# A transformer block with expert retrieval: the middle group's mixer spread over more tiles, and the score loads moved to ScalarE's DMA queue

## What is computed

```python
h = modulate(rmsnorm(x), shift1, scale1)
qa, ka, va, qb, kb, vb, ga, gb = split(h @ w_in)
y_sb = stick_breaking_attention(qa, ka, va)          # 8 heads, strictly causal
y_sw = sliding_window_sink_attention(qb, kb, vb)     # 8 query heads, 2 chunks of 64
x = x + gate1 * ((sigmoid(ga) * (y_sb @ sb_proj) + sigmoid(gb) * (y_sw @ sw_proj)) @ w_out)
h2 = modulate(rmsnorm(x), shift2, scale2)
# per token and head (8): scores against 2 x 128 sub-keys, top 16 of each,
# top 16 of the 256 sums, softmax over them
x = x + gate2 * sum_k gate_k * gelu(h2 . U[e_k]) * V[e_k]      # 128 experts of a token
out = rmsnorm(x)
```

## Time and profile before

| | |
|---|---|
| time, median of 3 runs | 3500.83 us (3499.89 to 3506.99) |
| the profiled execution's own time | 3481.42 us |
| its span | 3479.6 us |
| first gather starts | 378.0 us |
| busy: TensorE, VectorE, ScalarE, GpSimd | 2187.0, 2024.9, 1152.5, 1121.8 us |
| moved by DMA | 1274.27 MB, 366 GB/s over the span |

### The profile page before, as it was taken

How to read it: one execution, slowest core, us unless ns; L and a number is a source line. 1 busy time by engine, 2 the same in 40 slices (tenths; PEclk the granted TensorE clock), 3 DMA queues, 4 the chain that set the end, 5 groups by cost and what they waited for, 6 DMA issues and landing times.

```text
span 3479.6 us, 35550 instructions
## 1 busy us (share of the span) xinstructions
PE 2187.0 (63%) x11116; PEld 979.8 (28%) x11116; DVE 2024.9 (58%) x4779; ACT 1152.5 (33%) x3650; POOL 1121.8 (32%) x1033
## 2 busy tenths in 40 slices
PE   5878677668976856777667877774433443344333
PEld 2566533244433412232233432341100000000000
DVE  1021556665655465777586667556666666666644
ACT  2111335642222235666543223222322232223222
POOL 0000133323322232444333333333344344434442
PEclk9999888889987978988888988886665565665655
DMA  9433679988999898999999999999999999999998
GB/s 367 171 133 111 258 296 367 357 330 347 372 371 394 332 419 326 416 390 396 368 370 412 421 421 385 392 420 421 392 421 421 421 399 421 421 421 391 421 421 335
DMA packets 197214, 1274.27 MB, mean 366 GB/s; under 512 B 21192, under 2 KB 38632, under 8 KB 54048
## 3 DMA queue, kind: packets, MB, share of 16 engines
q0 software_dynamic: 147616, 1074.03, 75.7%
q1 hardware_dynamic: 49408, 197.96, 14.6%
HBM read 1247.51 MB, written 24.40 MB: 366 GB/s over the span
## 4 chain that ended last, share of the span: by engine, by line
PE 40%; DMA 35%; ACT 10%; issue 9%; DVE 5%; POOL 1%; SPq 0%; POOLq 0%; DVEq 0%; ACTq 0%
DMA arena<-in_uv,idx_r 26%; PE pb L969 13%; PE pb L752 5%; PE pb L684 5%; ACT dg L1206 3%; PE pb L714 3%; ACT L105 2%; PE pb L687 2%; PE pb L773 2%; DMA arena<-in_w_ada 2%; DMA arena<-in_w_q 2%; PE pb L955 2%; DVE arena L1524 2%; PE pb L848 1%; PE pb L659 1%
## 5 line engine op out<-in xcount | busy, mean ns | idle before, releaser
L606 POOL DMA_INDIRECT arena<-in_uv,idx_r x1024 | 1118.7, 1093 | 2329.7 <-PE pb L969 1719.5
L1524 DVE CUSTOM_DVE_ANT_0 arena<-arena 128x1024 f32<-128x1024 f32 x1024 | 1249.3, 1222 | 743.1 <-DMA arena<-in_uv,idx_r 703.6
L969 PE MATMUL pb<-arena,dg 128*32 128x512 f32 x4096 | 735.3, 855 | 866.6 <-ACT dg L1206 866.6
L969 PEld LDWEIGHTS pb<-arena,dg 128*32 128x32 f32 x4096 | 134.3, 138 | 1357.0 <-ACT dg L1206 1060.9
L1200 ACT ACTIVATE gl<-dots 128x4 f32<-128x4 f32 x256 | 52.4, 205 | 989.0 <-DVE dots L1524 987.9
L752 PE MATMUL pb<-arena 128*128 128x384 f32 (+1 forms) x768 | 250.7, 484 | 66.2 <-issue 51.8
L105 ACT ACT_TABLE_LOAD x177 | 227.1, 1283 | 133.1 <-DVE dots L1524 77.0
L684 PE MATMUL pb<-arena 128*128 128x384 f32 (+1 forms) x768 | 238.8, 465 | 15.9 <-DMA arena<-in_w_mg 15.2
L1206 ACT ACTIVATE dg<-ig,gl 128x32 f32<-128x32 f32 x1024 | 245.1, 310 | 8.4 <-ACT gl L1200 0.2
L1195 ACT ACTIVATE ig<-istack,gate_r 128x32 f32<-128x32 f32 x1024 | 241.6, 308 | 0.0
L752 PEld LDWEIGHTS pb<-arena 128*128 128x128 f32 x768 | 153.6, 205 | 158.6 <-issue 95.1
(11 more groups left out here) (156 smaller groups left out, 2232.4 us busy)
## 6 DMA issues: line engine op xcount, KB each, us to landing
arena<-in_w_mg SPq DMA_DIRECT2D x24, 1536.0 KB, 10.8
arena<-in_w_ada SPq DMA_DIRECT2D x12, 2048.0 KB, 17.3
arena<-in_w_q SPq DMA_DIRECT2D x24, 1024.0 KB, 12.7
arena<-in_uv,idx_r POOLq DMA_INDIRECT x1024, 12.0
arena<-in_w_qk SPq DMA_DIRECT2D x12, 1024.0 KB, 13.6
arena<-in_w_out SPq DMA_DIRECT2D x3, 4096.0 KB, 16.2
arena<-in_w_sw SPq DMA_DIRECT2D x3, 3072.0 KB, 11.6
arena<-in_x SPq DMA_DIRECT2D x16, 512.0 KB, 15.2
```

Source lines behind the costliest of these rows:

```text
L606: pool.indirect_dma_start(ring[:, i % RING, :], None, uv, bass.IndirectOffsetOnAxis(ap=idx_r[:, b % 2, 4 * n + c:4 * n + c + 1], axis=0)). ...
L969: m = pe.matmul(pb[32 * c:32 * c + 32, VACC + i, :], dg[:, STEP * n // 4 % 2, c, :], ring[:, (STEP * g + c - first) % RING, D + i * HALF:D ...
L1524: dve.tensor_tensor_reduce(u, h2rep[:, slot(b, c), :], u, 1.0, 0.0, ALU.mult, ALU.add, dots[:, i % 8:i % 8 + 1]).then_inc(dots_done, 1)
```

## The change

Three numbers of the plan and one generator change.

1. `RATES` goes from (1.9, 2.9, 1.9) to (1.9, 2.5, 2.1): group 1's stages from H to OUT are spread over more tiles, group 2's over fewer. Group 2's start is no longer fixed at tile 235 but follows 2 tiles after group 1's end.
2. `SPREAD = (4.7, 8.0, 9.0)` sets the tiles that one head of PREP takes. Before they followed from the rate: 4.7, 4.7 and 7.1.
3. Selection of chunk n starts at tile 32n - 52 (`LEAD`) in place of 32n - 64, if the scores are ready in the plan by then.
4. The load of a chunk's scores is a row of ScalarE's program, 10 tiles ahead of the selection in place of 1.5, or 1.5 tiles ahead of it when the scores are just ready.

Places in the plan, in tiles:

| | before | after |
|---|---|---|
| group 1: H, QK, SWP, MG, OUT, PREP | 0, 15.4, 78.6, 109.4, 155.0, 181.6 | 0, 17.2, 89.2, 124.4, 177.2, 206.8 |
| group 2: H, QK, SWP, MG, OUT, PREP | 235, 256.4, 389.6, 434.7, 504.2, 540.6 | 272.8, 292.5, 413.8, 455.0, 517.8, 551.6 |
| group 2 ends | 599 | 624 |
| chunk 8 (first of block 2): selected from, to | 194.3, 224.3 | 224.1, 254.1 |
| chunk 9: selected from, to | 224.0, 254.0 | 240.1, 270.1 |
| load of chunk 8, load of chunk 9 | 192.8, 222.5 | 222.6, 238.6 |

```diff
-RATES = (1.9, 2.9, 1.9)
+RATES = (1.9, 2.5, 2.1)
+SPREAD = (4.7, 8.0, 9.0)
+LEAD = 52
...
-            self.now = begins[g]
+            self.now = begins[g] if g < len(begins) else self.now + 2
...
-                self.item("PREP", g, h, 18 * part)
-            self.now += 2
+                self.item("PREP", g, h, SPREAD[g] * RATES[g])
...
-        at = Plan([-probe("PREP", 0, 2) - 36, 0.0, 235.0])
+        at = Plan([-probe("PREP", 0, 2) - 36, 0.0])
...
+        def ready_at(b, m):
+            return at("PREP", GROUP[b], 2 * m + 1, part(GROUP[b], 11) + 4)
+
         def topk_at(b, m):
             n = CHUNKS * b + m
-            ready = at("PREP", GROUP[b], 2 * m + 1, part(GROUP[b], 11) + 4)
-            return ready if n < 2 else max(32.0 * (n - 2), ready)
+            return ready_at(b, m) if n < 2 else max(32.0 * n - LEAD, ready_at(b, m))
...
-                            yield topk_at(b, m) - 1.5
+                            yield max(topk_at(b, m) - 10, ready_at(b, m) - 1.5)
                             done = 16 * (HEADS // 2 * GROUP[b] + m + 1)
-                            sp.wait_ge(s_st[0], done)
-                            sp.wait_ge(s_st[1], done)
+                            act.wait_ge(s_st[0], done)
+                            act.wait_ge(s_st[1], done)
                             if n >= 2:
-                                sp.wait_ge(tk_used, n - 1)
-                            sp.dma_start(tk[:, n % 2, :], ...).then_inc(in_tk[n % 2], 16)
+                                act.wait_ge(tk_used, n - 1)
+                            act.dma_start(tk[:, n % 2, :], ...).then_inc(in_tk[n % 2], 16)
```

More of the change, by code:

```diff
@@ L542, in parked @@
                                      ssb[h % 2][:, 0:GB].rearrange("p b q n -> p b (q n)")).then_inc(s_st[h % 2], 16)
[L544 to L549, removed]
-                            yield topk_at(b, m) - 1.5
-                            done = 16 * (HEADS // 2 * GROUP[b] + m + 1)
-                            sp.wait_ge(s_st[0], done)
-                            sp.wait_ge(s_st[1], done)
-                            if n >= 2:
-                                sp.wait_ge(tk_used, n - 1)
-                            sp.dma_start(tk[:, n % 2, :], s_dram[b, :, 2 * m:2 * m + 2, :].rearrange("p h n -> p (h n)")).then_inc(in_tk[n % 2], 16)
                 def blocks():
@@ L582, in finals @@
                         sp.dma_start(out[b * P:(b + 1) * P, :], yfin).then_inc(stored, 16)
-                interleave(start(), mods(), first_weights(), mixer(0), parked(0), keys(), blocks(), finals(), *[s for g in range(1, GROUPS) for s in (mixer(g), parked(g))])
+                interleave(start(), mods(), first_weights(), mixer(0), parked(0), blocks(), finals(), *[s for g in range(1, GROUPS) for s in (mixer(g), parked(g))])
                 sp.wait_ge(stored, 16 * NB)
@@ L1173, in gates, with keys @@
                                            pb[:, MISC, 0:64].rearrange("p (c a n) -> p c a n", c=4, a=2)[:, :, 1], ACT.Copy).then_inc(pub_g, 1)
+                def keys():
+                    for b in range(NB):
+                        for m in range(CHUNKS):
+                            n = CHUNKS * b + m
+                            if n == 0:
+                                continue
+                            yield max(topk_at(b, m) - 10, ready_at(b, m) - 1.5)
+                            done = 16 * (HEADS // 2 * GROUP[b] + m + 1)
+                            act.wait_ge(s_st[0], done)
+                            act.wait_ge(s_st[1], done)
+                            if n >= 2:
+                                act.wait_ge(tk_used, n - 1)
+                            act.dma_start(tk[:, n % 2, :], s_dram[b, :, 2 * m:2 * m + 2, :].rearrange("p h n -> p (h n)")).then_inc(in_tk[n % 2], 16)
                 def replicate():
@@ L1217, in final @@
                         act.activation(stats[:, 50:51], stats[:, 49:50], ACT.Sqrt).then_inc(fin_rstd, 1)
-                interleave(start(), gates(), replicate(), gelus(), final(), *[mixer(g) for g in range(GROUPS)])
+                interleave(start(), keys(), gates(), replicate(), gelus(), final(), *[mixer(g) for g in range(GROUPS)])
             @block.vector
```

## The result

| | before | changed |
|---|---|---|
| median | 3503.90 us, 4 runs (3499.89 to 3506.99) | 3425.84 us, 4 runs (3419.07 to 3428.72) |
| ratio, 95% interval | | 0.9775 (0.9755 to 0.9795) |
| profiled execution, span | 3481.42, 3479.6 us | 3426.72, 3424.9 us |
| first gather | 378.0 us | 380.3 us |

The two profiled executions differ by only 54.7 us. All medians are of executions in the fast state; a single one, 5929.01 us in the experiment at rate 2.4, was in the slow state and is left out.

What follows compares the result with a forecast made beforehand. Taken as bound by bytes at 420 GB/s plus 243 us lost time; 34 + 16 + 5 + 4 - 12 - 8 - 2 = 37 us less, so 3500.8 - 37 = 3464 us, range 3430 to 3505.

Steps and rivals of the forecast that it cites:

- 1.4 us won per tile moved into such a stretch: Engine-bound stretches: a tile adds 1.2 us, saves 2.6 elsewhere; 34 us won in group 1's H to OUT.
- The first 142 us: Group 1's H, V and wait for its first weights: under 2 tiles moved, so 0 won of 43.3 lost.
- 16 for PREP: Group 1's PREP grows from 37 to 64 tiles, query weights no longer waited for: 16 us won, 7 left lost.
- The 8 us for tile 256: GpSimd waits for tile 256's indices, then chunk 9's 24 rows stand in one piece: 8 us lost, 24 if uncovered.
- The two waits of ScalarE: At chunk 8's and 9's loads ScalarE waits 11 us twice for stores; covered by gathers, otherwise 22 us lost.
- rival (c): Slower: ScalarE's two store waits empty the queue in group 1's PREP; about 3534 us, 3507 with half the stalls; chance 0.12.
- -12 and +5: Group 2, H to OUT: 12 us lost for 25 fewer tiles, 5 won as chunk 10's score wait goes.
- The runs' median lies 19.4 us above that execution: Whole kernel: offset between profiled execution and timed runs carried along, so 3444 us profiled became 3464 us.
- (b): Large win: group 1 falls to group 2's loss of 0.15 us per tile, group 2 pays nothing; about 3436 us; chance 0.17.
- (a): Small win: a tile costs its path 2.0 us, group 2 pays what group 1 gains; about 3496 us; chance 0.17.
- (d): Clock: thinner mixer idles TensorE; group 1's MG and PREP clock falls from 0.95 to 0.8; about 3495 us; chance 0.04.
- (e): Whole kernel: nothing moves, since only the bytes count; chance 0.03 at most.

Runs made afterwards that it cites:

- experiment at rate 2.4: Changed kernel with group 2's rate raised from 2.1 to 2.4: 3429.05 us, ratio 0.9786 to the kernel before.
- plan alone: Kernel before with only the new rates, PREP's spread and group 2's start, loads still on SyncE, selection 64 tiles ahead: 3430.64 us, 0.9855; repeated 3429.44, 0.9844.
- 2.7: Kernel before with group 1 at rate 2.7 and eight tiles per head of its PREP, group 2 at 1.9, loads on SyncE: 3474.41 us, 0.9906.
- 2.5: Kernel before with group 1 at rate 2.5 and eight tiles per head of its PREP, group 2 at 1.9, loads on SyncE: 3466.19 us, 0.9890.
- PREP alone: Kernel before with eight tiles in place of 4.7 per head of group 1's PREP, group 1 staying at rate 2.9: 3495.60 us, 0.9975.
- its variants: Changed kernel with chunk 8's selection in 18 tiles, 3416.25 us; or with rates 1.9, 2.4, 2.0, spread 4.7, 7, 8 and chunk 8 in 22 tiles, 3461.59.
- The two experiments in which half the change was made: Kernel before with only the new rates, spread and group 2 start, 0.9855; or with only loads on ScalarE, 10 tiles ahead where scores allow, 0.9975.

## Why the prediction was wrong

**The frame held.** Bytes at 420 GB/s plus lost time gives both profiles; the sum of the ledger (54.5) is the difference of the profiled executions (54.7).

**The term that was mis-sized: "and so 1.4 us won per tile moved into such a stretch".** H to OUT of group 1 won 48.4 us in place of 34. In this pair it is 24 tiles more and 48.4 us less lost, 2.0 us a tile. The plan alone, set against the kernel before at the same level, gives 1.9. The step behind the term, 1.2 us of added path per tile, failed: 24 tiles made these stages 17.0 us longer, 0.7 us each (0.85 with the plan alone), the lower end that the prediction itself had named for TensorE alone, and 2.6 - 0.7 is 1.9. QK and SB even took 8 more tiles and got shorter by 3.6 us. So the path got longer by less than a tile's work on VectorE alone (1.2 us). One leg of the 1.2 was also misread: the earlier trace rows count 177 table loads in the whole kernel, 0.7 for every four tiles and not two, so ScalarE's work on a tile is some 0.7 us and not 1.2. The steps from 2.9 to 2.7 and to 2.5 agree on the first half (2.1 us a tile) and suggest that it doesn't stay so (0.6).

**"The first 142 us ... 0"** was 5.5 us.

**PREP and tile 256.** 16 for PREP was near (22.7 to 9.5 us in the changed kernel, to 7.1 with PREP alone). Its reason is shown in part. Behind the first head no query weights were waited for, as said, but the first head's took 12.0 us as before, and nothing was lost by leaving the loads on SyncE: the plan alone does as well in PREP. So the tiles closed that stretch, not the load's move. The 8 us for tile 256 were 2.5 by the windows.

**The two waits of ScalarE** came with 11.85 and 13.15 us where 11 stood, and cost nothing visible; rival (c) rests on them and is refuted.

**Group 2** paid 8.7 us in H to OUT in this pair, 3.3 by three profiles each, where -12 and +5 stood. The 4 us for its PREP didn't come, but 4.1 came in the rest: for group 2 and all behind it -6.4 in place of -3. The price of 12 was too high: with rate 1.9 restored nothing came back, and at 2.4 only 7 us went. (By the plan's places the stages lose 27 tiles and not 25.)

**The step that cost most: "The runs' median lies 19.4 us above that execution, so the time is 3500.8 - 37".** That took the distance for a thing that every kernel has between its profile and its runs. The changed kernel's median lies 0.9 us below its profiled execution, and in all 19 profiles taken after the prediction the distance is under 8 us. By its time and by the missing mark the profile of before was of the 3482 level, and its timed runs were of the 3504 level. So 17.5 of the 38 us by which the prediction missed lie in the sum, and 19 to 21 in this step. The two experiments in which half the change was made, both at 3482, give -52 and -7 (-53 and -4.5 in the repetition), together 57 to 59, close to the profiled pair's 54.7. The missing 20 appear only where the kernel before is at its upper level.

**What stays open.** The changed kernel was never run in a session at the 3482 level, so it isn't shown whether it would be faster there too, and by how much; nor which part of the change would make it insensitive to the level. The kernels with SyncE's loads at the upper level (PREP alone, 2.7, 2.5) lose 37 to 43 us in the part behind group 2, the changed kernel and its variants 25 to 28, with the mark in both. They differ in the selection's lead, in the loads and in the tiles for a head of group 2's PREP (7.1 and 9.0, or 8.0), and no run separates these at that level.

**The rivals.** (b) is nearest: in the stretches that it speaks of (520 to 1211 us before, 512 to 1273 in the changed kernel) the loss fell from 101 to 48 us, 53 of its 66, at 0.20 us per tile rather than 0.15. (a) is refuted in its reason: a tile cost its path 0.7 us where it said 2.0. (d) didn't come: TensorE's granted clock over the whole MG stage is 0.95 in both kernels, and in PREP 0.89 against 0.91; TensorE is busy for 2184.3 us in all, 2.7 less than before. (e) is refuted by the 78 us.

## What to carry to other kernels

Where a memory stream runs beside in-order engines, look for the stretches with the most lost time (length times one less the share of the full rate) and give them more of the stream, by spreading their other work thinner, even where an engine seems full: here a tile added to the tight stages made them 0.7 us longer, and 2.6 us were saved elsewhere. Waits shorter than what is in flight cost little here (11.85 and 14.27 us under up to ten gathers of 2.5 us), so neither the number nor the sum of waits prices a change. A ledger row of one pair of profiles can be off by several us, so take a second profile before reading a small one. And before a profile's time is set against a median, repeat the profile: if the two differ, they may be two levels of the same kernel, not an offset to be carried along.

## What the runs showed of the hardware

- One program ran at two levels on the same chip, each kept for a whole session: 3480.6 and 3503.1 us, with 12 runs each, with ScalarE's publication row 2 to 3 us later behind TensorE's last matmul at the upper one (2.7 in place of 0.4 us in the median).
- The DMA engines kept 419 and 398 GB/s in the 10 us windows in which GpSimd issued two and four gathers and otherwise stood for 14.27 us.
- Moving the 31 loads of 256 KB from SyncE's queue to ScalarE's with nothing else changed: ratio 1.0003 (0.9992 to 1.0015).
- TensorE's sum of a tile took 0.48 us in MG, where the granted clock was 0.95, and 0.7 us in the mean of the kernel, where it was 0.79.
- With the same number of tiles in QK and SB of group 1 (72), a kernel of other rates took 232.3 us there in place of 214.7. One and the same program took 219.8 us there at the lower level and 228.6 at the upper one.
